# Two-block model on one Trainium2 core: another order of the matmuls of the fast products, and of steps at either end of that stage

## The reference

```python
D_FF = -(-8 * D_MODEL // (3 * 256)) * 256            # 5632 = 44 tiles of 128
h = rmsnorm_2(x, g_pre_ffn[l]) * (1.0 + sc_f) + sh_f
f = (jax.nn.silu(h @ w_gate[l]) * (h @ w_up[l])) @ w_down[l]
x = x + gt_f * rmsnorm_2(f, g_post_ffn[l])
```

## Time and profile before

| | |
|---|---|
| median of three runs | 3108.85 us |
| the profiled execution | 3110.98 us |
| its span, first to last instruction | 3109.3 us |
| mean granted TensorE clock | 0.994 |
| PE busy | 3062.8 us of the span |
| PEld busy | 2561.6 us |
| DVE busy | 2163.4 us |
| ACT busy | 1158.3 us |
| fast products, from first to last start | 1801.2 to 2620.4 us |

### The profile page before, as it was taken

The page is one execution under the profiler, slowest core; times in us unless marked ns, Lnnn a source line. Parts: engine busy times, 40 slices in busy tenths (PEclk is TensorE's granted clock), DMA queues, the critical chain, the costliest instruction groups (busy, mean ns, idle before and its releaser), DMA issues.

```text
span 3109.3 us, 41520 instructions
## 1 busy us (share of the span) xinstructions
PE 3062.8 (99%) x15416; PEld 2561.6 (82%) x15416; DVE 2163.4 (70%) x2827; ACT 1158.3 (37%) x1522; POOL 345.0 (11%) x505
## 2 busy tenths in 40 slices
PE   8999999999999999999999899999999999999998
PEld 7888877888878888888887688888888888888887
DVE  6666656868885444555688888888888887666665
ACT  5233343213233333444432454444444444222223
POOL 0211100111100000000011300000000000112113
PEclk9999999999999999999999899999999999999999
DMA  5444454876762222222276456666666666454544
GB/s 187 148 124 132 130 196 156 316 262 219 262 251 82 82 81 81 82 82 76 108 274 253 155 158 177 175 175 175 175 175 175 175 175 210 176 190 176 193 172 164
DMA packets 118266, 525.00 MB, mean 169 GB/s; under 512 B 22080, under 2 KB 22352, under 8 KB 80912
## 3 DMA queue, kind: packets, MB, share of 16 engines
q1 hardware_dynamic: 63920, 321.15, 29.3%
q0 software_dynamic: 50352, 174.40, 19.2%
q10 hardware_dynamic: 3888, 28.03, 2.3%
HBM read 435.17 MB, written 37.76 MB: 152 GB/s over the span
## 4 chain that ended last, share of the span: by engine, by line
PE 96%; DVE 3%; DMA 0%; ACT 0%; DVEq 0%; issue 0%; ACTq 0%
PE PS L1724 18%; PE PS L1305 15%; PE PS L1307 15%; PE PS L1306 15%; PE PS L1727 9%; PE PS L1757 5%; PE PS L1756 5%; PE PS L1755 5%; PE PS L1574 1%; PE PS L1601 1%; PE PS L1358 1%; PE PS L1359 1%; PE PS L1360 1%; PE PS L1589 1%; PE PS L1471 0%; PE PS L1430 0%
## 5 line engine op out<-in xcount | busy, mean ns | idle before, releaser
L1305 PE MATMUL PS<-XHL,WH 128*128 128x512 f32 x1968 | 775.1, 394 | 6.4 <-DVE WL L1767 3.4
L1307 PE MATMUL PS<-XHL,WL 128*128 128x512 f32 x1968 | 766.2, 389 | 0.0
L1306 PE MATMUL PS<-XHL,WH 128*128 128x512 f32 x1968 | 766.0, 389 | 0.0
L812 ACT ACTIVATE WH<-RAW 128x2048 fp32r<-128x2048 f32 x138 | 263.9, 1912 | 525.8 <-PE PS L1307 516.7
L1305 PEld LDWEIGHTS PS<-XHL,WH 128*128 128x128 f32 x1968 | 369.4, 188 | 94.3 <-issue 14.2
L1307 PEld LDWEIGHTS PS<-XHL,WL 128*128 128x128 f32 x1968 | 369.4, 188 | 77.7
L1306 PEld LDWEIGHTS PS<-XHL,WH 128*128 128x128 f32 x1968 | 369.5, 188 | 76.9 <-issue 2.2
L1767 DVE TENSOR_TENSOR WL<-RAW,WH 128x2048 fp32r<-128x2048 f32 x138 | 316.5, 2294 | 80.9 <-ACT WH L812 80.8
L1150 ACT ACTIVATE QH<-RAW 128x1024 fp32r<-128x1024 f32 x210 | 222.4, 1059 | 254.4 <-PE PS L1727 250.2
L1724 PE MATMUL PS<-XHL,QH 128*128 128x512 f32 x1008 | 316.5, 395 | 0.0
L2594 DVE TENSOR_TENSOR QL<-RAW,QH 128x1024 fp32r<-128x1024 f32 x210 | 256.6, 1223 | 59.0 <-ACT QH L1150 58.9
(11 more groups left out here) (371 smaller groups left out, 4543.9 us busy)
## 6 DMA issues: line engine op xcount, KB each, us to landing
RAW<-w_units_dram SPq DMA_DIRECT2D x268, 1024.0 KB, 4.9
ADA<-w_ada_dram POOLq DMA_DIRECT2D x192, 512.0 KB, 5.6
SUM<-RAW POOLq DMA_DIRECT2D x42, 512.0 KB, 4.5
RAW<-SUM POOLq DMA_DIRECT2D x42, 512.0 KB, 4.5
FR<-f_dram SPq DMA_DIRECT2D x10, 1024.0 KB, 5.5
spill_dram<-SIG POOLq DMA_DIRECT2D x24, 256.0 KB, 2.3
f_dram<-TMP SPq DMA_DIRECT2D x22, 256.0 KB, 7.0
f_dram<-FO SPq DMA_DIRECT2D x22, 256.0 KB, 6.8
```

The source lines that it names most:

```text
L812: act.activation(WH[:, slot, :], RAW[:, slot, :], ACT.Copy).then_inc(hi_ready, 1)
L1305: pe.matmul(PS[:, bank, :], wh, rh[:, x, :], start=k == 0, stop=False)
L1306: pe.matmul(PS[:, bank, :], wh, rl[:, x, :], start=False, stop=False)
L1307: ins = pe.matmul(PS[:, bank, :], wl, rh[:, x, :], start=False, stop=k == n - 1)
```

## The change

In the fast products PE takes each tile of weights with its own low part at once: QH k, QL k, QH k+1, QL k+1. On DVE, ahead of the first fast product, `plain_hidden(1)` and the count on `copied` move two instructions forward, ahead of the low part for j = 1, and the low part for j = 3 moves behind the making of TC. On SP the last hidden tile is saved before the second chunk is loaded instead of after it; the load of that chunk then stands behind the wait for the last hidden tile. On DVE the first low part of that chunk, `hidden_lo(1, 0)`, moves from behind the third output read of chunk 0 to ahead of the first.

```diff
--- before.py
+++ after.py
@@ -482,16 +482,16 @@
             hidden_saved(FF_TILES - 2, f_d[FF_TILES - 2], 0)
             sp.wait_ge(x_ready, X_HID + FF_CHUNK)
             down_load(1)
+            hidden_saved(FF_TILES - 1, f_d[FF_TILES - 1], 1)
             for n in range(2, FF_TILES):
                 if n % 4 == 2 and n // 4 + 1 < FF_CHUNKS:
                     c = n // 4 + 1
                     if c == 1:
 
                         sp.wait_ge(q_done, Q0 + PRODUCTS * FAST)
+                        sp.wait_ge(f_made, FF_TILES)
                     sp.wait_ge(x_ready, X_HID + FF_CHUNK * c)
                     hidden_loaded(c)
-                    if c == 1:
-                        hidden_saved(FF_TILES - 1, f_d[FF_TILES - 1], 1)
                 sp.wait_ge(d_lo, n - 1)
                 down_load(n)
 
@@ -1719,14 +1719,13 @@
                         pe.wait_ge(copied, 3 * s + (COPIED0 + 2))
                     else:
                         pe.wait_ge(taken, 4 * s + (TAKEN0 + {1: -5, 2: -4, 4: -6, 6: 1}[j]))
-                    for k0 in range(0, FULL_K, 2):
-                        for k in (k0, k0 + 1):
-                            pe.matmul(in_halves(PS[:, bank, :]), QH[:, slot, k * P:(k + 1) * P], fast_data(j, k),
-                                      start=k == 0 and j not in (3, 5, 6), stop=False, skip_group_check=True)
-                        for k in (k0, k0 + 1):
-                            ins = pe.matmul(PS[:, bank, 0:HALF_S], QL[:, slot, k * P:(k + 1) * P],
-                                            fast_data(j, k)[:, HIGH.get(j, 0), :],
-                                            start=False, stop=k == FULL_K - 1, skip_group_check=True)
+                    for k in range(FULL_K):
+                        wh, wl = (w[:, slot, k * P:(k + 1) * P] for w in (QH, QL))
+                        x = fast_data(j, k)
+                        pe.matmul(in_halves(PS[:, bank, :]), wh, x, start=k == 0 and j not in (3, 5, 6), stop=False,
+                                  skip_group_check=True)
+                        ins = pe.matmul(PS[:, bank, 0:HALF_S], wl, x[:, HIGH.get(j, 0), :], start=False, stop=k == FULL_K - 1,
+                                        skip_group_check=True)
                     ins.then_inc(q_done, 1)
 
             pair(U_FFN, O_FFN, X_FFN)
@@ -2686,18 +2685,18 @@
             ins.then_inc(t_lo, 1)
             sum_3(0, 32)
             lo_part(0, 0, 0, 0)
+            plain_hidden(1)
+            v.drain().then_inc(copied, 1)
             lo_part(0, 0, 1, 1)
             sum_1(0)
-            plain_hidden(1)
-            v.drain().then_inc(copied, 1)
             lo_part(0, 0, 2, 2)
-            lo_part(0, 0, 3, 3)
             v.wait_ge(t_hi, 3)
             for t in range(FULL_K):
                 m = 3 * DT + FULL_K + t
                 ins = v.scalar_tensor_tensor(out=TC[:, t, hi], in0=RES[:, FULL_K + t, hi], scalar=MOD[:, m:m + 1],
                                              in1=f32(TC[:, t, lo]), op0=ALU.add, op1=ALU.subtract)
             ins.then_inc(t_lo, 1)
+            lo_part(0, 0, 3, 3)
             lo_part(0, 0, 4, 0)
             v.wait_ge(t_hi, 4)
             v.tensor_tensor(TB[:, :, lo], RES[:, a, lo], f32(TB[:, :, hi]), ALU.subtract).then_inc(t_lo, 1)
@@ -2719,7 +2718,7 @@
             for n in range(FF_TILES - 2):
                 c, m = divmod(n, FF_CHUNK)
                 down_lo(n + 1)
-                if 1 <= n and c + 1 < FF_CHUNKS:
+                if c + 1 < FF_CHUNKS:
                     hidden_lo(c + 1, m)
                 if n in ADA_DOWN:
                     ada_chunk(ADA_DOWN[n])
@@ -2737,8 +2736,6 @@
                 v.drain()
                 for b in range(4):
                     down_read(c, 4 * m + b)
-                    if n == 0 and b == 2:
-                        hidden_lo(1, 0)
             down_lo(FF_TILES - 1)
 
             def scale(b):
```

## The result

The changed kernel takes 3130.72 us (median of 4 runs, 3128.41 to 3134.07), the kernel before 3109.91 (4 runs, 3108.54 to 3112.80). The ratio on record is 1.0055, 95% interval 1.003 to 1.0081, that of the medians 1.0067. The record lists twelve executions of the changed kernel in all: ten took 3127.39 to 3134.07 us and two took 3113.93 and 3114.30, which fits the lower ratio. In the experiments two executions, 14665.62 us of the kernel with the matmul order alone changed and 7220.72 us of the kernel before, were far slower than all others and are left out of the medians and ratios. The profiled execution took 3130.39 us, its span 3128.7. The forecast was 3113.5, range 3107 to 3121. The direction was right, the size and the range were wrong.

What follows compares the result with a forecast made beforehand. PE was taken as the bound, busy 3062.8 of 3109.3 us. Terms 0 + 2.6 + 2.05 = +4.65 us, called 4.7, on the median of 3108.85 gave 3113.5 us, range 3107 to 3121.

Steps and rivals of the forecast that it cites:

- Bound and slack: Fast and down stages: matmul rate sets the end; other engines cost nothing until PE waits, then every us counts.
- Part 1: Fast products, matmuls one by one: same count of matmuls, weight loads and columns, only neighbours differ; 0 us.
- holds each kind of neighbour: Fast products: reason for taking 0, the present group has every transition and half of them are those left.
- The bound (+27.8): Fast products: if all 23.6 ns a group belong to changes of width, 1176 groups grow by 27.8 us.
- a change of width costs PE: Rival, fast products: at 3 ns a pair it adds 7.1 us, 3120.6; at the bound 3141; chance 0.20.
- The rival that alternating gains: Fast products: alternating gives each weight load a wide matmul's slack; 3.5 ns a pair faster gives 3105.3; chance 0.12.
- The 23.6 ns that I called unexplained: Fast products: a group of two pairs takes 696.6 ns against a floor taken as 673.0.
- Part 2: Start of the fast stage: DVE's new order makes its steps late and PE wait, +2.6 us.
- terms 0.5, 1.5 and 0.6: Start of the fast stage: us by which products 2, 3 and 6 of pair 0 begin late.
- Part 3: Start of the down stage: FR, issued 3.36 us later, delays the fifth output; PE stall +2.05 us.
- the 9.4 that was the upper end: Down stage: FR's longest landing, us, taken from the weight load issued in that slot; stall then 4.45 us.
- Slower by over 0.2%: Whole kernel: measured time slower than 3115.07 us, beyond what a measurement can tell from no change; chance 0.40.

Runs made afterwards that it cites:

- the run alone: Kernel before with only DVE's order ahead of the first fast product changed; ratio 1.0007 (0.9998 to 1.0016), fast stage 821.92 us.
- two others: Kernel before with only SP's and DVE's down-stage steps changed, 3115.16 us; changed kernel with only its matmul order taken back, 3119.26 us.
- pe_mirror: Kernel before with fast matmuls in mirrored runs of two (QH 0, QL 0, QL 1, QH 1); 3111.36 us against 3110.21, one run.

## Why the prediction was wrong

- **Bound and slack: right.** Each wait on PE and each ns of its rate reached the end.
- **Part 1, the matmul order, 0: this step failed.** It measured +11.8 us, the larger part of the 19.4 between the profiles. With the two stalls as they measured and part 1 at 0 the time would have been 3108.85 + 8.9 = 3117.8, within the range; so the direction came out right by the stalls, and the miss is this term. The argument counted weight loads under narrow matmuls, and the count is indeed the same. What costs is how matmuls of unlike width are grouped: 353.3 ns a pair in runs of one, 348.3 in runs of two. The step that failed is to take the present group as a measure of the new order because it "holds each kind of neighbour". It did not follow, since the sum over four transitions doesn't tell the cost of the two that are left; and it isn't so, since the runs of 3, 4 and 8 show that the cost is no sum over neighbours at all. The bound (+27.8) held it, and the rival "a change of width costs PE" (0.20) named the place with 3 ns a pair instead of 5.0. But its form was wrong too: a price per change would make runs of eight the fastest, and they lose to runs of two. The rival that alternating gains (0.12) had the sign wrong: within a run of eight narrow matmuls, each with its own load, the spacing stays at 120.0 and no delay builds up; the loss stands in the wide ones behind them. The 23.6 ns that I called unexplained were measured from too low a floor: narrow matmuls in a steady run take 120.0 ns, not the 109.8 of 128 columns (in a row whose weight tiles have only 16 columns, though full tiles show 109 too), and the present order lost only 3.3 ns a group. It was near its floor of 346.7 ns a pair, so a large gain was never to be had, and a loss was. That the plain units give 226.7 for 512 columns, 13.4 above 512 columns at 2.4 GHz, suggests 106.7 + 13.4 = 120.1 for 256, which is what was measured; it was no rule to rely on beforehand, since 128 columns would come to 66.7 by it and take 109.8. By the Trainium skill (TensorE: Matmul & The Clock Gate, Back-to-back issue gap) that addition is 2.5 ns; with a new weight tile for each matmul these runs show 13.3.
- **Part 2, +2.6: right**, 2.4 in the changed kernel and 2.65 alone. Of the terms 0.5, 1.5 and 0.6 the run alone shows 0.52, 1.52 and 0.49 from start to start, the changed kernel 0.44, 1.47 and 0.39. The brackets show less, 0.3, 1.2 and 0.3, because a matmul counts as busy for 0.16 us beyond the start of the next; I should have forecast the lateness and not the wait.
- **Part 3, +2.05: mechanism right, mis-sized**, 6.5 in the changed kernel, 5.3 and 7.2 in two others. Two terms failed. FR's landing was taken at 7.0; it took 8.6 to 9.6 with the save ahead, and in the changed kernel 9.6, above the 9.4 that was the upper end, and the fifth output began 2.7 us later than forecast for it. And the clock was left out: after waits of 2.71 to 4.56 us in this place it was at the lower level, which cost 1.7 us more in three traces and 2.8 in the fourth. After the wait of 1.70 us it was not. The sharing of the DMA engines among queues, which the Trainium skill states (DMA: Bandwidth & Descriptors, Queues, rings and completion order), fits a longer flight beside the loads of TIN, but no run here proves it. The prediction's estimate from this page of the Trainium skill gave the save in SP's own ring 1.4 us of flight; the traces allow 0.3 to 1.4, and the medians with and without it, +5.4 and +5.6, show no difference.
- **Chances.** "Slower by over 0.2%" had 0.40. The range left out the outer half of the rival on width, for which I had the least evidence: its 3 ns a pair gave 3120.6, its measured 5.0 would have given 3125.3. A mechanism that is unmeasured and multiplied by 2352 should have had its bound in the range.

## What to carry to other kernels

Where PE is the bound, the order of its matmuls is worth a measurement even when no instruction is added: a few ns times thousands. Mixing 512 and 256 columns cost least here in runs of two; take no rule for other lengths from one of them. A wait that is added to a DMA queue sets several transfers off at one moment; look for what else waits for that semaphore. And price a wait of PE with the clock behind it: here 1.7 to 2.8 us on top of waits of 2.71 us and more.

## What the hardware showed that I had not expected

- With its own weights each, matmuls of 512 columns start every 226.7 ns and matmuls of 256 every 120.0, both 13.3 ns above the columns at 2.4 GHz. Mixed, the loss per round trip is 6.7, 3.3, 10.0, 16.7 and 20.0 ns for runs of 1, 2, 3, 4 and 8. It is not monotonic, and in runs of 2, 4 and 8 every product repeats it to 1 ns. What inside TensorE makes it is open: no run here separates the reading of data, the load of weights and the writing of results.
- Right after a change the narrow matmuls follow faster than in a steady run (113 ns) and the wide ones slower (up to 236, in runs of one up to 241). So in these traces the spacing of two or three starts is no measure of the rate.
- The granted clock was at its lower level after idle times of 2.71, 3.50, 4.18 and 4.56 us at this place, and at the upper after 1.70 us. The number of matmuls with spacings above 0.3 us did not follow the length: 10 after 2.71 us, 8 after 3.50, 13 after 4.18, 9 after 4.56. Nor does the length alone decide whether it falls. Near 1655 us, between plain units, the traces have another wait of PE. In the kernel before it lasted 3.44 us and the clock stayed at 1.00; in pe_mirror it lasted 2.39 us and the clock was 0.50 after it. The rows of PE and the windows that follow them, first of the kernel before, then of pe_mirror:

```profile
1655.62 0.47 PE L1305 MATMUL PS<-XHL,WH 128*128 128x512 f32 x1 [3.44 <-DVE WL L1767]
1656.00:1658.00 2.00, 2.00 (x10) 1.62 (x9) 2.00 (x5) 0.00 (x0) 0.53 (x1) 1.00 0.69 164
```

```profile
1654.51 0.76 PE L1305 MATMUL PS<-XHL,WH 128*128 128x512 f32 x1 [2.39 <-DVE WL L1768]
1655.00:1657.00 2.00, 2.00 (x6) 1.54 (x5) 2.00 (x5) 0.14 (x1) 0.53 (x1) 0.50 0.72 213
```

No variant here is faster than the kernel before.
